# A new order for the plain weight pairs of four gated stages, and two of four weight sums made by adding transfers in all of them

## What is computed

```python
def swiglu(x, w_gate, w_up, w_down):
    return (jax.nn.silu(x @ w_gate) * (x @ w_up)) @ w_down
```

```python
def conv_ffn(y, w_up, conv_w, conv_b, w_down):
    up = y @ w_up
    u, v = jnp.split(up, 2, axis=-1)
    u_pad = jnp.pad(u, ((0, 0), (CONV_WIDTH - 1, 0), (0, 0)))
    c = conv_b
    for j in range(CONV_WIDTH):
        c = c + conv_w[j] * u_pad[:, j:j + S]
    return (jax.nn.gelu(c, approximate=False) * v) @ w_down
```

## Time and profile before

| | us |
|---|---|
| median of 3 runs | 2063.9 |
| lowest, highest | 2063.21, 2068.07 |
| the profiled execution's own time | 2059.96 |
| its span | 2058.2 |
| PE busy | 2016.5 (98%) |
| VectorE busy | 1460.7 (71%) |
| ScalarE busy | 986.3 (48%) |
| POOL busy | 245.7 (12%) |

### The profile page before, as it was taken

One profiled execution on the slowest core, in us unless ns is written; L12 is line 12 of the kernel. 1 busy time (PEld: TensorE's weight loads), 2 busy tenths in 40 slices (PEclk: granted clock), 3 DMA queues, 4 the chain that ended last, 5 costly groups with the idle time before them and its releaser, 6 DMA issues.

```text
span 2058.2 us, 32611 instructions
## 1 busy us (share of the span) xinstructions
PE 2016.5 (98%) x12670; PEld 1763.5 (86%) x12670; DVE 1460.7 (71%) x2427; ACT 986.3 (48%) x1607; POOL 245.7 (12%) x266
## 2 busy tenths in 40 slices
PE   9999999999999999999999899999999999899998
PEld 7899988778899988988787799888877797899887
DVE  7888833886888853687877888833667777888733
ACT  5455622354355542463554455622567753555522
POOL 0000000400000000000020122000446420122001
PEclk9999999999999999999999999999999999999999
DMA  8322233312232222322222476332357523566332
GB/s 254 122 103 103 89 101 110 119 64 82 88 118 103 90 92 89 123 92 71 67 80 90 132 184 182 110 109 97 115 143 173 146 83 103 164 178 178 93 97 69
DMA packets 90141, 236.99 MB, mean 115 GB/s; under 512 B 47728, under 2 KB 51104, under 8 KB 73616
## 3 DMA queue, kind: packets, MB, share of 16 engines
q1 hardware_dynamic: 72896, 184.04, 27.3%
q0 software_dynamic: 14768, 37.49, 8.4%
q10 hardware_dynamic: 2336, 13.52, 1.9%
HBM read 211.86 MB, written 7.38 MB: 107 GB/s over the span
## 4 chain that ended last, share of the span: by engine, by line
PE 79%; DVE 13%; ACT 3%; DMA 2%; issue 2%; POOL 0%; SPq 0%; DVEq 0%; ACTq 0%
PE ps L1279 25%; PE ps L1280 24%; PE ps L1281 24%; DVE w_lo L1781 1%; DVE xq L2555 1%; DMA raw<-raw 1%; DVE act L2513 1%; ACT xq L2029 1%; PE ps L511 1%; DVE xq L2537 1%; PE ps L524 1%; PE ps L735 1%; PE ps L717 1%; DMA w_sum<-in_w_up 1%; DVE w_lo L1771 1%
## 5 line engine op out<-in xcount | busy, mean ns | idle before, releaser
L1781 DVE TENSOR_TENSOR w_lo<-raw,w_hi 128x2048 fp32r<-128x2048 f32 (+3 forms) x144 | 287.8, 1999 | 170.0 <-ACT w_hi L1753 161.9
L1279 PE MATMUL ps<-act,w_hi 128*128 128x512 f32 (+1 forms) x1026 | 376.5, 367 | 4.2 <-DVE act L2513 1.8
L1280 PE MATMUL ps<-act,w_hi 128*128 128x512 f32 (+1 forms) x1026 | 371.9, 362 | 0.0
L1281 PE MATMUL ps<-act,w_lo 128*128 128x512 f32 (+1 forms) x1026 | 371.8, 362 | 0.0
L1279 PE MATMUL ps<-xq,w_hi 128*128 128x256 f32 x1024 | 292.8, 286 | 13.0 <-issue 12.6
L1280 PE MATMUL ps<-xq,w_hi 128*128 128x256 f32 x1024 | 291.6, 285 | 0.0
L1281 PE MATMUL ps<-xq,w_lo 128*128 128x256 f32 x1024 | 291.6, 285 | 0.0
L1279 PEld LDWEIGHTS ps<-act,w_hi 128*128 128x128 f32 x1026 | 193.5, 189 | 43.0 <-issue 7.6
L1279 PE MATMUL ps<-xq,w_sum_hi 128*128 128x256 f32 x768 | 218.1, 284 | 5.0 <-ACT prod L1997 3.2
L1281 PEld LDWEIGHTS ps<-act,w_lo 128*128 128x128 f32 x1026 | 193.5, 189 | 30.0
L1280 PEld LDWEIGHTS ps<-act,w_hi 128*128 128x128 f32 x1026 | 193.7, 189 | 28.9
(11 more groups left out here) (297 smaller groups left out, 4016.0 us busy)
## 6 DMA issues: line engine op xcount, KB each, us to landing
raw<-in_w_up SPq DMA_DIRECT2D x87, 1024.0 KB, 4.8
raw<-in_w_down SPq DMA_DIRECT2D x29, 768.0 KB, 4.2
raw<-in_w_in SPq DMA_DIRECT2D x20, 1024.0 KB, 4.7
raw<-in_w_down SPq DMA_DIRECT2D x29, 640.0 KB, 3.9
w_sum<-in_w_up POOLq DMA_DIRECT2D x64, 256.0 KB, 3.8
raw<-in_w_out SPq DMA_DIRECT2D x8, 1024.0 KB, 4.8
raw<-raw POOLq DMA_DIRECT2D x32, 256.0 KB, 4.9
raw<-in_w_in ACTq DMA_DIRECT2D x8, 1024.0 KB, 4.8
```

The lines of the kernel that those rows point to most:

```text
L1279: pe.matmul(own, hi, rhs_hi, start=start, stop=False, skip_group_check=more)
L1280: pe.matmul(own, hi, rhs_lo, start=False, stop=False, skip_group_check=more)
L1281: return pe.matmul(own, lo, rhs_hi, start=False, stop=stop, skip_group_check=more)
L1781: eng.tensor_tensor(w_lo[:, w], raw[:, w], w_hi[:, w].bitcast(F32), ALU.subtract).then_inc(lo_rounded, 1)
```

## The change

- DVE's work for a plain pair is written out in `plain_dve`, ACT's in `plain_act`. The up bank is evacuated straight to `own_act(f)` (the product's own place) and no longer waits for the last product; instead the gate's evacuation waits for the last activation or tap.
- The product of pair 0 comes behind w_lo of pair 3; the product of pair 1 behind the quarters. In a conv stage the quarter sums move into pairs 2 and 3 (in halves), in a silu stage they stay in pair 1.
- w_hi and w_lo of pair 3 are made in pair 1's turn in all four stages; w_hi of pair 5 comes before the xq roundings.
- The xq roundings are spread over pairs 3 and 4, and the four rests over pairs 3, 4 and 5, each with its own count of `xq_ready`; PE waits for each piece only before the quarter product that reads it.
- Weight sums of pair 6 are made in pair 3's turn, its rests in pairs 4 and 5.
- Pair 5's tap, activation and product move behind pair 6's first steps.
- `stats_at` goes from 5 to 3 in up3 and up4.
- `sums_by_transfer` runs for all four stages; `sum_pair` makes one sum instead of three in up1 and up2.

The diff, cut to its core:

```diff
         def summed(st, f, count):
-            n, whole = seven_index(st, f), 2 * (KF - PLAIN)
-            return 4 * n + count if n < whole else 4 * whole + 2 * (n - whole) + count - 2
+            return 2 * seven_index(st, f) + count - 2
...
+                rests = 4 * SEVEN.index(st.name)
                 if f == PLAIN:
-                    pe.wait_ge(xq_ready, SEVEN.index(st.name) + 1)
+                    pe.wait_ge(xq_ready, rests + 1)
                 quarter(ra, of_pair(0), 0, True).then_inc(seven_done, 1)
+                if f == PLAIN:
+                    pe.wait_ge(xq_ready, rests + 2)
                 quarter(rc, of_pair(4), 2, True).then_inc(seven_done, 1)
+                if f == PLAIN:
+                    pe.wait_ge(xq_ready, rests + 3)
...
-                    stats_at = 2 if st.name == "up2" else 5
+                    stats_at = {"up1": 5, "up2": 2, "up3": 3, "up4": 3}[st.name]
...
+            def plain_act(st, f, f0):
+                a, conv = SEVEN.index(st.name), st.evac == "conv"
+                if 0 < f < PLAIN - 2:
+                    round_weights(eng, st.q0 + f + 2, 0, 0)
+                if f == PLAIN - 2:
+                    round_pair_summed(st, PLAIN)
+                    round_sum(st, PLAIN, 0)
+                if conv and f < PLAIN - 1:
+                    first_tap(st, f)
+                if f == PLAIN - 3:
+                    round_quarters(a, 0)
+                if f == PLAIN - 2:
+                    round_sum(st, PLAIN, 1)
+                    round_sum(st, PLAIN, 2)
+                if f < PLAIN - 1:
+                    silu(f, f0)
+                if f == PLAIN - 3:
+                    round_quarters(a, 1)
+                if f == PLAIN - 2:
+                    round_quarters(a, 2, 3)
...
                 keep(prod[:, 0:HALF], ra, 6 * n + 1)
+                if f == PLAIN and st.evac == "silu":
+                    silu(f - 1, f0)
+                if f == PLAIN and st.evac == "conv":
+                    first_tap(st, f - 1)
...
                 keep(up[:, 0:HALF], ra, 6 * n + 3)
+                if f == PLAIN and st.evac == "conv":
+                    silu(f - 1, f0)
...
             def sum_pair(st, f):
-                if st.evac == "conv":
-                    eng.wait_ge(third_landed, 16 * (n - 2 * (KF - PLAIN) + 1))
-                else:
-                    eng.wait_ge(raw_landed[q % 2], 16 * (q // 2 + 1))
-                    eng.tensor_tensor(quad(w_sum, 1), g1, u1, ALU.add).then_inc(w_summed, 1)
-                    eng.wait_ge(w_summed, summed(st, f, 1))
-                    eng.tensor_tensor(u1, u1, u2, ALU.add).then_inc(w_summed, 1)
-                    eng.wait_ge(w_summed, summed(st, f, 2))
+                eng.wait_ge(third_landed, 16 * (n + 1))
                 eng.tensor_tensor(quad(w_sum, 0), g1, u1, ALU.add).then_inc(w_summed, 1)
...
+            def plain_dve(st, f, f0):
+                conv = st.evac == "conv"
+                b = 5 if f == 0 else 2 * ((st.g0 + f) % 2)
+                eng.wait_ge(pair_done, st.q0 + f + 1)
+                if conv:
+                    wait(eng, gate_ready, f0 + f)
+                    eng.tensor_tensor(shifted[:, 2:], bank(b), rstd[:, :], ALU.mult).then_inc(u_ready, 1)
+                else:
+                    wait(eng, gated_ready, f0 + f)
+                    eng.tensor_tensor(gate[:, :], bank(b), rstd[:, :], ALU.mult).then_inc(gate_ready, 1)
+                eng.tensor_tensor(own_act(f), bank(b + 1), rstd[:, :], ALU.mult).then_inc(evacuated, 1)
+                if f == 3 and conv:
+                    sum_quarters(st, 1)
+                if 0 < f < PLAIN - 2:
+                    rest_weights(eng, st.q0 + f + 2, 0, 0)
+                if f == PLAIN - 2:
+                    rest_weights(eng, st.q0 + PLAIN, 0, 0)
+                    rest_sum(st, PLAIN, 0)
+                if f == 1:
+                    gated_product(st, 0, f0)
+                if conv and f < PLAIN - 1:
+                    other_taps(st, f)
+                if f == 1:
+                    scaled_quarters(st)
+                    if not conv:
+                        sum_quarters(st, 0)
+                        sum_quarters(st, 1)
+                if f == 2 and conv:
+                    sum_quarters(st, 0)
+                if f == PLAIN - 2:
+                    rest_quarters(st, 1)
+                if 0 < f < PLAIN - 1:
+                    gated_product(st, f, f0)
+                if f == PLAIN - 3:
+                    sum_pair(st, PLAIN)
+                    fourth_sum(st, PLAIN)
+                    rest_quarters(st, 0)
+                if f == PLAIN - 2:
+                    rest_quarters(st, 2)
+                    rest_sum(st, PLAIN, 1)
+                if f == PLAIN - 1:
+                    rest_quarters(st, 3)
+                    rest_sum(st, PLAIN, 2)
...
             for st in stages:
-                if st.name in ("up3", "up4"):
+                if st.name in SEVEN:
                     for f in range(PLAIN, KF):
                         sums_by_transfer(st, f)
```

More of the change, by code:

```diff
@@ L1582, in seven_pe @@
                 pe.wait_ge(fourth_ready, n + 1)
+                if f == PLAIN:
+                    pe.wait_ge(xq_ready, rests + 4)
                 quarter(ra, of_pair(12), 6, False).then_inc(pair_done, 1)
@@ L1985, in round_sum @@
                 n = seven_index(st, f)
-                if st.evac == "conv" and c == 1:
-                    eng.wait_ge(fifth_landed, 16 * (n - 2 * (KF - PLAIN) + 1))
+                if c == 1:
+                    eng.wait_ge(fifth_landed, 16 * (n + 1))
                 else:
@@ L2010, in round_act, with round_quarters @@
                 eng.activation(chunk(act, act_hi(f)), own_act(f), ACT.Copy).then_inc(prod_hi, 1)
+            def round_quarters(a, *groups):
+                for j in groups:
+                    eng.wait_ge(xq_sum, a + 1)
+                    c, count = 2 * j, min(2, 7 - 2 * j)
+                    eng.activation(xq[:, xq_hi_at(c, count)], xq32[:, xq_lo_at(c, count)], ACT.Copy).then_inc(xq_hi_ready, 1)
+            def plain_act(st, f, f0):
[18 more added lines that the diff above has]
+                    round_quarters(a, 2, 3)
             def seven_act(st, f, f0):
@@ L2015, in seven_act @@
                 if f < PLAIN:
[L2016 to L2029, removed]
+                    plain_act(st, f, f0)
                     return
@@ L2594, in conv_dve @@
                 eng.wait_ge(seven_done, 6 * n + 5)
-                wait(eng, prod_ready, f0 + f)
+                wait(eng, prod_ready, f0 + f if f > PLAIN else f0)
                 eng.tensor_tensor(up[:, HALF:T], ra, prod[:, HALF:T], ALU.add).then_inc(fourth_ready, 1)
@@ L2608, in seven_dve @@
             def seven_dve(st, f, f0):
                 if f < PLAIN:
-                    b = 5 if f == 0 else 2 * ((st.g0 + f) % 2)
-                    eng.wait_ge(pair_done, st.q0 + f + 1)
-                    if st.evac == "conv":
-                        eng.tensor_tensor(shifted[:, 2:], bank(b), rstd[:, :], ALU.mult).then_inc(u_ready, 1)
-                    else:
-                        eng.tensor_tensor(gate[:, :], bank(b), rstd[:, :], ALU.mult).then_inc(gate_ready, 1)
-                    wait(eng, prod_ready, f0 + f)
@@ L2618, in seven_dve @@
-                    eng.tensor_tensor(up[:, :], bank(b + 1), rstd[:, :], ALU.mult).then_inc(evacuated, 1)
-                    if plain_rounding(st, f):
-                        rest_weights(eng, st.q0 + plain_rounding(st, f), 0, 0)
-                    if st.evac == "conv":
-                        other_taps(st, f)
-                    if f == PLAIN - 2:
-                        sum_pair(st, PLAIN)
-                        fourth_sum(st, PLAIN)
-                        rest_weights(eng, st.q0 + PLAIN, 0, 0)
-                        for c in range(3):
-                            rest_sum(st, PLAIN, c)
```

64 lines of the change are left out of this document (27 added, 37 removed).

## The result

| | us |
|---|---|
| changed kernel, median of 4 runs | 2039.82 (2035.17 to 2047.62) |
| kernel before, median of 4 runs on the same chip | 2065.24 (2063.21 to 2068.07) |
| ratio | 0.988, 95% interval 0.9843 to 0.9916 |
| profiled execution of the changed kernel | 2035.17, span 2033.4 |

The changed kernel is faster by 1.2%. Its median lies 1.5 us under the 2041.3 forecast, and inside the range. Lines of code have moved: PE's products are L1272 to L1274 (before L1279 to L1281), the mean is L1259 (L1266), an adding transfer is issued by L2987 (L2951).

What follows compares the result with a forecast made beforehand. PE, busy 2016.5 of 2058.2 us, was taken as the bound. Terms -23.4 (up3, up4), +0.9 (up1), -0.75 (up2) and +0.6 (steady pairs) sum to -22.65 on 2063.9: 2041.3 us, range 2035 to 2050.

Steps and rivals of the forecast that it cites:

- The two long waits: Openings of up3 and up4: PE's waits of 3.43 and 6.07 us go, winning 11.7 us a stage, 23.4 together.
- The walk: New order stepped through DVE, ACT, PE and POOL for up3 with trace durations; pair 7 begins at 1155.0 against 1166.73.
- The reason given for the two waits: up3, up4: VectorE makes scaled quarters with sums, and the four rests (7.8 us), each in one piece ahead of needed work.
- Inside pair 6: up3, up4: sixth quarter waits 0.9 us for ACT's third copy, seventh 1.9 us for fourth_ready.
- rival B: up3, up4: the clock still falls in pair 6, costing 3 us in both, total 2044; chance 0.14.
- +0.9 forecast: up1: DVE waits for the adding transfer, landing at 65.8; pair 7 begins at 89.0 against 88.09, 0.9 us lost.
- The estimate by the Trainium skill: up1: 2.6 us for a 256 KB transfer, sum landing at 63.5, term -1.4 in place of +0.9, total 2039.0.
- -0.75 forecast: up2: pair 6 starts without loss, waits 0.4 us inside instead of 1.15, pair 7 at 575.3 against 576.06.
- Steady pairs: up1, up2, fifteen pairs each: fewer DVE sums worth nothing, three more transfers a pair cost 0.3 us a stage, bounds 0 and 1.3.
- rival C: Long landings: up1's adding transfer takes 8.3 us, steady pairs of up1 and up2 lose 1.3 a stage; total 2047; chance 0.13.
- rival D: POOL's transfer cycle becomes the period of up1 and up2, slower than before; 2071 at 1.0 us a pair; chance 0.05.
- rival E: up3, up4 openings stay late because a step counted as hidden holds DVE; no change, 2058 to 2062; chance 0.08.

Runs made afterwards that it cites:

- early_sums: Changed kernel with the four quarter sums of up3 and up4 back in pair 1's turn, ahead of w_lo of pair 4; one run, pair 7 of up3 0.77 us later.
- whole_rests: Changed kernel with the quarters' roundings and rests each in one piece again, w_hi of pair 5 still ahead of the roundings; one run, 2038.42 us.
- late_product: Changed kernel with pair 5's product moved behind fourth_ready of pair 6 in up3 and up4; 2044.27 us, two late pairs of up1 and up2 included.
- stats4: Changed kernel with the mean behind k=4 instead of k=3 in up3 and up4, and pair 5's product behind fourth_ready of pair 6; 2038.25 us, ratio 0.9893.
- early_up: Changed kernel with w_lo of pair 7 and pair 5's product behind fourth_ready of pair 6 in up3 and up4; 2040.95 us, ratio 0.9887.
- transfers_only: Kernel before, old order kept, with two of the four weight sums made by adding transfers in up1 and up2 too; 2060.89 us, ratio 1.000.
- double_sum: Changed kernel with one quarter sum of up3 and up4 made twice on VectorE; pair 7 of up3 1.25 us later, of up4 1.27.
- order_only: Changed kernel with all four weight sums of up1 and up2 made on VectorE again, the new order kept; 2035.35 us, ratio 0.9875.
- again: The changed kernel itself, unedited, measured once more in more rounds; 2035.87 us, ratio 0.9879.
- best: early_up with up1's four weight sums made on VectorE again, the other stages by transfers; 2037.98 us, ratio 0.9873.

## Why the prediction was right

**The two long waits.** The sum's main term, 11.7 a conv stage, was measured at 11.55 and 11.81. The steps in between held too. up3's pair 1 begins 0.93 earlier on the trace of after, so 0.93 is added for the comparison: mean 1091.9 (forecast 1091.8), pair 2 1098.85 (1098.5), pair 6 1142.4 (1142.2), pair 7 1155.2 (1155.0). w_lo of pair 4 is done at 1115.8, and PE takes pair 4 at 1119.68: 3.9 us to spare (forecast 4). The walk worked because all that it needed were durations of the earlier trace rows, which did not change: w_lo takes 2.28 on DVE in both.

**The reason given for the two waits.** The forecast put them on two blocks of DVE work, each made in one piece. This reason is mostly not borne out, though the walk didn't rest on it. With either block put back, 0.8 us a stage return (early_sums, whole_rests). What the walk also had, and the reason left out, is w_hi of pair 5 ahead of ScalarE's roundings (6.26 us of DVE's idle time) and the mean 2.7 us earlier (1.73).

**Inside pair 6.** 0.9 and 1.9 were forecast; 0.65 and 1.57 are the waits, 0.90 and 1.83 counted from start to start with the slower matmul behind each, which is the whole of 12.81 - 10.08. The step that was right in number and too narrow in meaning is this one: I read them as two late steps. The experiments show that they are the end of DVE's queue: none of the three reorderings tried (late_product, stats4, early_up) wins them. The change turned an opening in which DVE stood idle for 11.65 us into one in which DVE's work itself is the limit.

**The clock (rival B, 0.14).** It stays at 1.00 behind these waits. One of 3.2 us in up1 of transfers_only does bring it down, as those of 3.4 and 6.1 did before. In the thirteen profiled executions the shortest single wait with a fall to 0.50 behind it is 2.38 us (double_sum, at 1187.7), the longest without one 1.81 (early_up, at 1873.9). The window begins with the first matmul behind the wait of 3.2:

```profile
93.50:97.00 3.50, 3.45 (x17) 3.45 (x18) 3.08 (x3) 1.37 (x3) 0.25 (x1) 0.54 0.99 171
```

**up1 (+0.9 forecast, -0.7 measured).** The mechanism was right, and the size of one step was not: the landing of the adding transfer. DVE does wait for the adding transfer, and has 21.6 us of work from there to fourth_ready (21.7 forecast; fourth_ready at 84.93). The landing was early: POOL's issue and DVE's sum in the changed kernel:

```profile
59.44 0.93 POOL L2987 DMA_DIRECT2D raw<-raw  x1 [32.89 <-DMA raw<-in_w_up]
...
63.36 0.70 DVE L2508 TENSOR_TENSOR w_sum<-raw 128x512 f32<-128x512 f32 x1 [5.75 <-DMA raw<-raw]
```

The raw weights were there at 59.4, not 60.6, and the transfer took 3.9 us where I took the median of 4.9: 63.4 in place of 65.8. Pair 7 came at 86.52, 2.5 us ahead of the 89.0 forecast; 0.84 of this is counted above as the earlier start of the program. Against order_only (22.83) the transfer costs 0.4 us here and 0.6 in again, so the direction of the term was right; the gain of 0.7 is the order's 1.2 less these 0.4. The estimate by the Trainium skill ("DMA: Bandwidth & Descriptors", "Anatomy of one DMA") had 63.5 for this point and 2039.0 for the whole. It came nearer, though with an error that cancelled: its 2.6 us for such a transfer is less than any landing here, whose least is 3.2 in the changed kernel.

**up2 (-0.75 forecast, -1.04 measured).** Pair 6 has no wait longer than 0.1 us inside; pair 7 takes over at 575.09. The forecast didn't say which part of the change wins this. The order alone loses 0.7 here (order_only), and the transfers win 1.7: two sums less in DVE's queue.

**Steady pairs (0.3 a stage, bounds 0 and 1.3; rival C, 0.13).** Of the 30 pairs 7 to 21 of up1 and up2, 29 take as long as before, and one takes 0.95 longer. So POOL's cycle is not the period (rival D, 0.05), and in these pairs DVE's shorter work (busy 1460.7 before, 1418.6 after, over the span) brought nothing, as forecast. But the term was mis-sized as a mean. In 21 stages with these transfers (up1 and up2 of all the profiled executions but those without them), eight pairs were late, by 0.9 to 5.3 us, in all 28: 1.3 us a stage, the top of my bound. The five stages that make the sums on DVE (two of before, two of order_only, one of best) had none. The runs' spread fits, 1.1 us over four runs of order_only and 12.5 over four of the changed kernel, but it proves little: the changed kernel spread by 3.9 as again, and the kernel before, without these transfers, by 8.9 over 17 runs.

**The conv openings (rival E, 0.08)** did not stay late: nothing in the stricter line held DVE up but the 0.70 us.

## What to carry to other kernels

When PE waits 6 us for work that another engine could have done earlier, write out that engine's queue with the durations of the trace; such a walk placed pairs 2, 6 and 7 of the new order within 0.4 us. When the waits have shrunk to 1 or 2 us, look in the feeding engine's timeline for idle time: if there is none, moving steps won nothing in the three cases tried here, and only less work or an earlier start counts, here a short wait on PE (0.73 us for the mean) that started DVE 1.7 us sooner. If there is idle time, ask what stands ahead of the missing operand in the other engine's list: here 6.26 us came from one rounding placed behind four others. Work taken off an engine that holds nobody up, as DVE in the steady pairs, is worth nothing, and paid for in transfers it brings a rare long wait.

## What was not expected of the hardware

A landing of an adding transfer (256 KB, raw<-raw) is of one of two kinds: of 752 in the thirteen profiled executions, 619 took less than 6.5 us, 6 took 6.5 to 7.0, and 127 took more. The changed kernel's transfers, and those of early_sums (duration of POOL's issue, and landing, least, median and most):

```profile
L2987 POOL DMA_DIRECT2D raw<-raw x64: 859/1193/1219, 59.4 to 1871.8; - x64
...
DMA to landing us min/median/max: 3.2/4.7/8.7
```

```profile
DMA to landing us min/median/max: 3.3/4.8/11.7
```

The longest one, in up2 of early_sums: POOL issues it, SP issues a load of 1 MB (raw<-in_w_up) half a us later, ACT waits for it with w_hi, and PE behind ACT.

```profile
600.29 1.17 POOL L2982 DMA_DIRECT2D raw<-raw  x1
...
600.83 0.34 SPq L1193 DMA_DIRECT2D raw<-in_w_up  x1
...
612.00 1.91 ACT L1978 ACTIVATE w_hi<-raw 128x2048 fp32r<-128x2048 f32 x1 [5.38 <-DMA raw<-raw]
...
614.23 0.58 PE L1272 MATMUL ps<-xq,w_sum_hi 128*128 128x256 f32 x1 [3.78 <-ACT up L1994]
```

The load landed with it, after 11.0 us where its median is 5.0. Which transfers are long can be counted from the issue and landing times, by how long behind the transfer's issue the next load of weights is issued:

| next load issued | transfers | over 7 us |
|---|---|---|
| within 2.0 us | 133 | 113 |
| 2.0 to 2.5 us | 131 | 13 |
| later | 488 | 1 |

So a long landing goes with a load issued within some 2 us of the transfer; with one issued later than 2.5 us it is rare, though the load is still issued while most of these transfers are under way. The load is late too: behind the 119 transfers with a load of up weights within 2.0 us its median landing is 6.7 us, behind the others 5.1. This is a count over executions, not an experiment: no run shifts the load on purpose.

The Trainium skill ("SBUF — State Buffer", "SBUF: two separate sides") says that VectorE can lock GpSimd out of the port through which it writes descriptors. The trace doesn't show it as the cause here: the issue of the 11.7 us transfer took POOL 1.17 us, the median issue 1.19, and the time passes behind it.
